# Two decoder layers on one core: early attention scores in the second layer, residual rows of the output projection written by ScalarE, and a block table for the compressed scores

## The chip, the core and the metric

The kernel runs on one core of one Trainium2 chip. A core has five engines that run their own instruction streams and meet at semaphores: TensorE (PE in the profile, with its weight loads as PEld), VectorE (DVE), ScalarE (ACT), GpSimd (POOL) and SyncE (SP), which here only issues DMAs. The metric is the time of one execution on the device in microseconds (us). Before the change the median of three runs is 758.22 us (757.21 to 758.95).

## The reference, cut to what matters

There are 256 tokens of width 1024 and two layers. Each layer is a token mixer followed by a mixture of 16 experts, and after each of the two stands a layer norm of `alpha * x + sublayer(x)`, with alpha = 4 ** 0.25.

```python
# layer 0: 16 heads of 64; keys and values in 4 groups
o_cmp = softmax(q @ kc^T, masked) @ vc     # kc, vc: 15 compressed blocks of keys and values for each group
o_slc = softmax(q @ ks^T, causal) @ vs     # all selected blocks are taken at this length
o_win = softmax(q @ kw^T, causal) @ vw     # the window covers all keys at this length
mix   = (g0 * o_cmp + g1 * o_slc + g2 * o_win) @ w_out
# layer 1: 16 heads, causal attention over one block
mix   = softmax(q @ k^T, causal) @ v @ w_out
# both layers
x = layer_norm(alpha * x + mix)
x = layer_norm(alpha * x + grouped_moe(x))     # two experts of 16 for each token, router by group
```

## The kernel before, in words

The tokens lie in two tiles of 128 rows. Weights stream through a ring of eight slots in SBUF (and a ninth place); SyncE issues each load when the slot's last user has signalled. The order in which SyncE issues is one fixed list: the projection weights of layer 0, its output weights, the first six expert matrices, then, after the output projection has freed its slots, the rest of the experts; layer 1 in the same way.

**Projection.** A unit is 512 columns of a projection weight, in eight chunks of 128 rows (index j). ScalarE rounds a chunk into a high part (`split_hi`, L1086), VectorE forms the low part (`split_lo`, L1416), and TensorE multiplies both (`project`, L579 to L581: six matmuls a chunk). There are three buffers of high and low parts, so a split waits until the chunk three before it has been used. In layer 1 the last unit (i == 5 in the loops) makes the second half of the values. After each unit two rotated tiles are transposed by TensorE (L618) and copied by ScalarE (`tr_copy`, L1099). The first half of the values is copied out of PSUM by ScalarE (`values`, L1215), the second half by VectorE (L1758).

**Attention.** The work is a row of items, 12 in layer 0 and 8 in layer 1, and every engine goes through them in a fixed order written out by hand. For each item m: TensorE writes the mask (L640) and adds the scores (L652) in two PSUM banks; VectorE takes the maximum (`attention_max`, L1465); ScalarE takes the exponential with its sum (L1235); VectorE makes the coefficient (`coefficients`, L1499); GpSimd scales the probabilities (L1348); TensorE transposes them (`transpose_probs`, L666) into PSUM banks 4 and 5; VectorE copies them to SBUF (L1748); TensorE multiplies by the values (`times_v`, L691 in layer 0, L696 in layer 1); VectorE collects the finished heads (`collect`, L1516 to L1519). In step m of its loop TensorE does scores(m), times_v(m - 3), transpose_probs(m - 2) and mask(m + 1). In layer 1 the masks and scores of items 0 and 1 are put ahead of the last chunk (j == 7) of the last unit.

**The compressed branch of layer 0** is woven into the first steps: at step 1 `compressed_scores` (L719) computes 32 small products, for each token tile, head pair and head: 64 rows of queries against 16 compressed keys. VectorE takes the maximum and subtracts it (L1473, L1474), ScalarE exponentiates (L1244), VectorE scales at step 2 (`compressed_scale`, L1480 to L1486, five instructions), TensorE transposes at step 3 (L728), VectorE copies at step 4 (L1490), and `times_compressed` (L704) adds the product to the heads' bank from step 4 on.

**The output projection's weights of layer 0** are split for w = 0 and 1 and j = 0 to 5 during the attention: ScalarE rounds (L1241), GpSimd (L1351) or VectorE (L1765) makes the low part.

**Output projection** (`mix_out`). Banks 0 to 3 hold tile a and half w. First `seed` (L784) writes alpha times the residual rows into each bank by a product with a scaled identity, at the two steps after the last item; one such product is two PE instructions. Then 8 products per bank add the projection: in layer 0 the first six as three fast products of split operands each (L777 to L779), the last two, and all eight of layer 1, as plain fp32 products (L774, two PE instructions each). At the third step after the last item TensorE does the first six of bank 0 in one go, before times_v of the last item:

```python
elif m < n + T:
    pe.wait_ge(L.exp, base[l].exp + m - 1)
    for w in range(2):
        seed(2 * (m - n) + w, m - n, w, False)
else:
    mix_out(l, 0, 0, range(0, 6))
```

Then come layer norm, routing and eight pairs of experts (`experts`), where the same kind of identity product (L784) puts the residual rows in banks 4 to 7.

Of the kernel before, what the change touches and what calls it, by code (L numbers as in the profile page):

```python
# [90 lines left out]
def build(nc, x, consts, w_in0, w_out0, cmp_kw1, cmp_kw2, cmp_vw1, cmp_vw2, cmp_kpos, cmp_vpos,  # L91
          w_in1, w_out1, router_w, router_b, w_gate, w_up, w_down, ln_g, ln_b, ln_cols, out):
    ctx = ExitStack()
    with ctx:
# [84 lines left out]
        kcT = R4[:, D + 768:D + 832]  # L179
# [58 lines left out]
        wo_hi, wo_lo = sem("wo_hi"), sem("wo_lo")  # L238
        bconst, blank = sem("bconst"), sem("blank")
# [118 lines left out]
        ITEMS = [12, 8]  # L358
        tile_of = lambda l, m: min(m % 3, 1) if l == 0 else m % T
# [23 lines left out]
        def wo_chunks(l, m):  # L383
            first = sum(WO_AT[:m])
            return list(enumerate(WO))[first:first + WO_AT[m]] if l == 0 else []

# [157 lines left out]
        def _(pe):  # L544
# [15 lines left out]
            def project(l, i):  # L560
# [64 lines left out]
            def mask(l, m):  # L625
                B = base[l]
                t, n, many = tile_of(l, m), keys(l, m), segs(l, m)
                if m == 0:
                    pe.wait_ge(L.tr_copied, B.tr_copied + (5, 8)[l])
                    pe.wait_ge(bconst, 3)  # L630
# [38 lines left out]
            def times_v(l, m):  # L669
# [30 lines left out]
                last.then_inc(L.pv, 1)  # L700

            def times_compressed(jq):
                pe.wait_ge(c_t_sb, 1)
                mm(ps[:, 6 + jq // 2 % 2, jq % 2 * S:(jq % 2 + 1) * S],  # L704
                   vblk[jq // 4][:, 2 * (jq % 4):2 * (jq % 4) + 2].rearrange("p i c -> p (i c)"), PTc[:, jq // 4, :],
                   start=False, stop=True, skip_group_check=True)

            def compressed_scores():
                pe.wait_ge(kct_sb, 1)
                pe.wait_ge(v_blocks, 1)  # L710
                for a in range(2):
                    mm(ps[:, 6 + a, 0:T * P], identb[:, :], bc(cmaskb[:, :, :], 2, H // 2), start=True, stop=False,
                       skip_group_check=True)
                for t in range(T):
                    for jq in range(H // 2):
                        for a in range(2):
                            h, g = slice(64 * a, 64 * a + 64), 2 * (jq // 4) + a
                            at = t * P + jq * CS
                            last = mm(ps[:, 6 + a, at:at + CS], qT[h, jq, t * P:(t + 1) * P], kcT[h, g * CS:(g + 1) * CS],  # L719
                                      start=False, stop=True, skip_group_check=True)  # L720
# [10 lines left out]
            def attention(l):  # L731
# [3 lines left out]
                for m in range(n + 3):  # L735
# [13 lines left out]
                    if 2 <= m < n + 2:  # L749
                        transpose_probs(l, m - 2)  # L750
                    if l == 0 and m == 3:
                        compressed_probs_transposed()
                    if l == 0 and m >= 4:
                        g, r = divmod(m - 3, 3)
                        if r == 0 or r == 1 and g == 0:
                            times_compressed(2 * g)
                        if r == 1:
                            times_compressed(2 * g + 1)
                    if (0, 1)[l] <= m < n - 1:
                        mask(l, m + 1)  # L760

            def mix_out(l, a, w, js):
                B, u = base[l], OUT[2 * l + w]
                if l == 0 and a == 0 and w == 0 and js.start == 0:
                    pe.wait_ge(wo_lo, len(WO))
# [199 lines left out]
            pe.wait_ge(blank, 2)  # L965
# [112 lines left out]
        def _(act):  # L1078
# [67 lines left out]
            for l in range(2):  # L1146
                B, C = base[l], rbase[l]
                def x_hi(a, ws=range(2)):
# [25 lines left out]
                if l == 0:  # L1174
# [36 lines left out]
                    copy(kcT, ps[:, 7, 256:320]).then_inc(kct_sb, 1)  # L1211
                else:
# [12 lines left out]
                n = ITEMS[l]  # L1225
                for m in range(n):
                    act.wait_ge(L.mx, B.mx + m + 1)
                    if m >= 2 and (l == 0 or m % T == 0):
                        act.wait_ge(L.pt, B.pt + m - 1)
                    if m >= 4 and l and m % T:  # L1230
                        act.wait_ge(L.pt, B.pt + m - 3)
                    k = keys(l, m)
                    for a in range(2):
                        for x in range(segs(l, m)):
                            last = nc.scalar.activation(probs(l, m)[:, a, x], ps[:, score_bank(l, m) + a, x * k:(x + 1) * k], ACT.Exp,  # L1235
                                                        bias=nmax[:, m % 2, a, x:x + 1],
                                                        accum_out=sums[:, m % 3, a, x:x + 1])
                    last.then_inc(L.exp, 1)
# [58 lines left out]
        def _(pool):  # L1297
# [36 lines left out]
            step(nc.gpsimd.memset(half, -0.5))  # L1334
            for l in range(2):
# [10 lines left out]
                for m in range(ITEMS[l]):  # L1346
                    pool.wait_ge(L.coef, B.coef + m + 1)
                    tt(probs(l, m), probs(l, m), bc(coef[:, m % 3, :, 0:segs(l, m)], 3, keys(l, m)), ALU.mult).then_inc(L.scaled, 1)  # L1348
                    for n, (w, j) in wo_chunks(l, m)[:1]:
                        pool.wait_ge(wo_hi, n + 1)  # L1350
                        tt(wo_lo_at(w, j), in_slot(("unit", OUT[w]))[:, j * UNIT:(j + 1) * UNIT], WO_HI[w][j],  # L1351
                           ALU.subtract).then_inc(wo_lo, 1)
# [37 lines left out]
        def _(dve):  # L1390
# [78 lines left out]
            def compressed_less_max():  # L1469
                dve.wait_ge(c_scored, 1)  # L1470
                scores_ = ps[:, 6:8, 0:T * P].rearrange("p a (k n) -> p a k n", n=CS)
                pairs = lambda v: v.rearrange("p (k a) -> p a k", a=2)
                step(nc.vector.tensor_reduce(pairs(cmax), scores_, AX.X, ALU.max, negate=True))  # L1473
                tt(Pc.rearrange("p (k a n) -> p a k n", a=2, n=CS), scores_, bc(pairs(cmax), 3, CS), ALU.add  # L1474
                   ).then_inc(c_less, 1)
# [218 lines left out]
            nc.vector.memset(identb[:, :], 0.0).then_inc(blank, 1)  # L1694
            nc.vector.memset(causalb[:, :], 0.0).then_inc(blank, 1)
            for l in range(2):
# [48 lines left out]
                for m in range(n + 4):  # L1745
                    if 3 <= m < n + 3:
                        dve.wait_ge(L.pt, B.pt + m - 2)
                        copy(probs_t(l, m - 3), ps[:, 4:6, 0:segs(l, m - 3) * keys(l, m - 3)]).then_inc(L.pt_sb, 1)  # L1748
                    if l == 0 and m == 4:
# [5 lines left out]
                    if l == 1 and m == 1:  # L1755
# [5 lines left out]
                    if l == 0 and m == 2:  # L1761
                        compressed_scale()
                    for c, (w, j) in wo_chunks(l, m - 1)[1:] if 1 <= m <= n else []:
                        dve.wait_ge(wo_hi, c + 1)
                        tt(wo_lo_at(w, j), in_slot(("unit", OUT[w]))[:, j * UNIT:(j + 1) * UNIT], WO_HI[w][j],  # L1765
                           ALU.subtract).then_inc(wo_lo, 1)
# [79 lines left out]
```

## Time and profile before

| | us |
|---|---|
| median of three runs | 758.22 |
| the profiled execution | 758.38 |
| its span | 756.6 |
| TensorE busy in it | 728.7 (96%) |
| VectorE, ScalarE, GpSimd busy | 295.8, 189.7, 109.2 |

The granted TensorE clock of the profiled execution is 0.995 of full speed. The page cuts the span into 40 slices of some 19 us. The DMA row of it is near 9 tenths in slices 1 to 5, near nothing in slices 6 and 7 (layer 0's attention), high through the experts, low again in slices 26 to 28 (layer 1's attention), and high to the end. On the time axis: layer 0's projections to about 84 us, its attention to 147, output projection and routing to 182, experts to 391; layer 1's projections to 470, its attention to 499, output projection and routing to 538, experts to the end.

### The profile page before, as it was taken

To read this page: it belongs to the slowest core of one execution; us is meant where nothing else is said; L and a number is where in the kernel's file an instruction comes from. 1 tells how busy PE (TensorE), PEld (TensorE's weight loads), DVE (VectorE), ACT (ScalarE), POOL (GpSimd) and SP (SyncE) were. 2 spreads that over 40 slices of the span, in tenths; PEclk is the share of its full clock that TensorE was granted. 3 is DMA by queue.
4 is the path that set the end of the run, shared out by engine and by line. 5 is a ranking of instruction groups with operands and counts; after the bars stand their busy time and mean duration, and the time that the engine had idled before them with its cause. 6 is when DMAs were issued, how large, how long until landed. Compare 5 with 4: busy or idle time off the path is not lost.

```text
span 756.6 us, 9076 instructions
## 1 busy us (share of the span) xinstructions
PE 728.7 (96%) x3740; PEld 391.6 (52%) x3740; DVE 295.8 (39%) x532; ACT 189.7 (25%) x435; POOL 109.2 (14%) x88
## 2 busy tenths in 40 slices
PE   8999978999999999999999999999999999999994
PEld 4877755676343443443247887646534344434331
DVE  4384788456221212121155786625421212112114
ACT  5343657133101101110132546503210111011001
POOL 0011267312000000000023230501200000000001
PEclk9999999999999999999999999999999999999997
DMA  9999800137999999999999976014799999999992
GB/s 329 299 381 424 351 1 1 57 112 272 379 407 432 426 426 427 427 427 421 422 395 386 407 287 223 1 56 158 302 376 422 429 426 429 428 429 427 420 421 112
DMA packets 42700, 245.06 MB, mean 324 GB/s; under 512 B 5920, under 2 KB 10144, under 8 KB 29344
## 3 DMA queue, kind: packets, MB, share of 16 engines
q1 hardware_dynamic: 42656, 244.43, 80.2%
q8 instruction: 32, 0.52, 0.3%
q14 instruction: 12, 0.10, 0.0%
HBM read 243.37 MB, written 1.05 MB: 323 GB/s over the span
## 4 chain that ended last, share of the span: by engine, by line
PE 79%; DMA 9%; DVE 7%; ACT 2%; issue 1%; POOL 1%; SPq 0%; DVEq 0%; ACTq 0%
PE ps L854 25%; PE ps L875 13%; DMA ring<-in_w_up 7%; PE ps L774 5%; PE ps L579 4%; PE ps L581 4%; PE ps L580 4%; PE ps L839 3%; PE ps L885 3%; PE ps L666 2%; PE ps L784 2%; PE ps L691 1%; DMA ring<-in_w_in 1%; PE ps L830 1%; PE ps L652 1%
## 5 line engine op out<-in xcount | busy, mean ns | idle before, releaser
L854 PE MATMUL ps<-ring,R 128*64 128x512 f32 x928 | 227.1, 595 | 0.0
L854 PEld LDWEIGHTS ps<-ring,R 128*64 128x64 f32 x928 | 70.2, 137 | 108.8 <-issue 107.2
L875 PE MATMUL ps<-ring,R 128*64 128x512 f32 x448 | 113.6, 596 | 0.0
L1108 ACT ACTIVATE wh<-ps,small 128x512 fp32r<-128x512 f32 x32 | 22.0, 688 | 264.4 <-PE ps L875 262.8
L1416 DVE TENSOR_TENSOR wl_r<-ring,wh 128x512 fp32r<-128x512 f32 x72 | 55.7, 792 | 41.4 <-ACT wh L1086 41.0
L875 PEld LDWEIGHTS ps<-ring,R 128*64 128x64 f32 x448 | 35.1, 137 | 67.1 <-issue 64.0
L1642 DVE SCALAR_TENSOR_TENSOR wl_r<-ps,small,wh 128x512 fp32r<-128x512 f32 x32 | 24.0, 751 | 104.8 <-ACT wh L1108 104.1
L579 PE MATMUL ps<-wh,xh_r 128*128 128x512 f32 x144 | 57.3, 398 | 1.1 <-DVE wl_r L1416 1.0
L1631 DVE TENSOR_TENSOR R<-R,ps 128x512 f32<-128x512 f32 x16 | 17.2, 1074 | 104.3 <-PE ps L854 104.3
L1086 ACT CAST wh<-ring 128x512 fp32r<-128x512 f32 x72 | 44.5, 623 | 51.5 <-PE ps L581 50.7
L581 PE MATMUL ps<-wh,xl 128*128 128x512 f32 x144 | 56.2, 390 | 0.0
L580 PE MATMUL ps<-wl_r,xh_r 128*128 128x512 f32 x144 | 56.1, 390 | 0.0
L1314 POOL TENSOR_TENSOR R<-wh,small 128x512 f32<-128x512 f32 x8 | 8.4, 1048 | 281.8 <-PE ps L860 266.8
L1638 DVE TENSOR_SCALAR wl_r<-ps 128x256 fp32r<-128x256 f32 x16 | 6.8, 425 | 104.5 <-PE ps L860 104.5
L1235 ACT ACTIVATE R<-ps,small 128x128 f32<-128x128 f32 (+1 forms) x96 | 39.1, 427 | 25.1 <-PE ps L666 17.9
L854 PE MATMUL ps<-R 128*64 128x512 f32 x96 | 42.9, 596 | 2.4 <-DMA ring<-in_w_up 2.4
L1348 POOL TENSOR_TENSOR R<-R,small 128x1024 f32<-128x1024 f32 (+1 forms) x20 | 34.5, 1726 | 45.6 <-DVE small L1499 25.3
L1340 POOL TENSOR_TENSOR R<-R 128x512 f32<-128x512 f32 (+1 forms) x16 | 22.9, 1434 | 109.1 <-DVE R L1459 109.1
L774 PE MATMUL ps<-ring,R 128*128 128x512 f32 x80 | 36.2, 595 | 0.0
L1105 ACT ACTIVATE R<-ps 128x512 f32<-128x512 f32 x16 | 9.6, 597 | 99.9 <-PE ps L854 99.9
L579 PEld LDWEIGHTS ps<-wh,xh_r 128*128 128x128 f32 x144 | 27.0, 188 | 8.8 <-DVE wl_r L1416 3.0
L581 PEld LDWEIGHTS ps<-wh,xl 128*128 128x128 f32 x144 | 27.0, 188 | 5.8
(219 smaller groups left out, 1001.7 us busy)
## 6 DMA issues: line engine op xcount, KB each, us to landing
ring<-in_w_gate SPq DMA_DIRECT2D x28, 2048.0 KB, 17.8
ring<-in_w_up SPq DMA_DIRECT2D x22, 2048.0 KB, 18.0
ring<-in_w_down SPq DMA_DIRECT2D x22, 2048.0 KB, 20.3
ring<-in_w_in SPq DMA_DIRECT2D x21, 1024.0 KB, 14.2
ring<-in_w_out SPq DMA_DIRECT2D x8, 1024.0 KB, 15.0
R<-in_w_up SPq DMA_DIRECT2D x4, 2048.0 KB, 17.5
R<-in_w_down SPq DMA_DIRECT2D x4, 2048.0 KB, 19.2
ring<-in_w_gate SPq DMA_DIRECT2D x8, 1024.0 KB, 25.5
```

What stands on the lines that cost most here:

```text
L579: mm(to, xh[:, j, tok], wh[:, c % WBUF], start=(j == 0), stop=False)
L580: mm(to, xh[:, j, tok], wl[:, c % WBUF], start=False, stop=False)
L581: last = mm(to, xl[:, j, tok], wh[:, c % WBUF], start=False, stop=(j == KJ - 1))
L774: last = mm(to, OT[j][:, tok], in_slot(("unit", u))[:, j * UNIT:(j + 1) * UNIT], start=False, stop=(j == KJ - 1), skip_group_check=True)
L854: last = mm(ps[64 * e:64 * e + 64, to, :], xe[:, j, at + 64 * e:at + 64 * e + 64], slots[e][:, j * UNIT:(j + 1) * UNIT], start=(j == 0), s ...
L875: last = mm(ps[64 * e:64 * e + 64, 2 + w, :], hT[:, k, 64 * e:64 * e + 64], slots[e][:, at:at + UNIT], start=(k == 0), stop=(k == FJ - 1))
L1086: copy(wh[:, c % WBUF], in_slot(("unit", u))[:, j * UNIT:(j + 1) * UNIT]).then_inc(w_hi, 1)
L1235: last = nc.scalar.activation(probs(l, m)[:, a, x], ps[:, score_bank(l, m) + a, x * k:(x + 1) * k], ACT.Exp, bias=nmax[:, m % 2, a, x:x + ...
L1340: tt(stage[r % 2][:, 0:n], stage[r % 2][:, 0:n], rope_b[r % 2][:, 0:n], ALU.add).then_inc(L.roped, 1)
L1348: tt(probs(l, m), probs(l, m), bc(coef[:, m % 3, :, 0:segs(l, m)], 3, keys(l, m)), ALU.mult).then_inc(L.scaled, 1)
L1416: tt(wl[:, c % WBUF], in_slot(("unit", u))[:, j * UNIT:(j + 1) * UNIT], wh[:, c % WBUF], ALU.subtract).then_inc(w_lo, 1)
L1642: stt(Yp[1][w], ps[:, 2 + w, :], slot_gate, Yp[0][w], ALU.mult, ALU.subtract).then_inc(rd.y_lo, 1)
```

## The change

Four edits, of which the last word of the title, "experts' identity products kept", says that `seed` stays in the experts.

1. **Residual rows by ScalarE.** After the exponentials of each layer's last two items ScalarE writes alpha times two half rows from SBUF into PSUM banks that those exponentials have just freed. TensorE's four `seed` products per layer go, and the first six products of bank 0 are spread over the three steps after the last item, two at each, all ahead of that step's times_v. `mix_out` waits for `seeded`, and in layer 0 for the low parts of its own half only. In layer 1, item 6 used only half of each of its two banks; two small products with the mask fill the other half there.
2. **Early scores in layer 1.** In the last unit, masks and scores of items 0, 1 and 2 go ahead of chunks 2, 4 and 6, and transpose_probs of item 0 ahead of chunk 7. ScalarE copies the first values at chunks 0 and 1 and does the exponentials of items 0 and 1 after the splits of chunks 4 and 6; VectorE does the maxima of items 0 and 1 after the splits of chunks 3 and 5, and the coefficient of item 0 after chunk 7. The loops then begin at item 2 or step 3.
3. **Compressed scores by a block table.** The compressed keys are kept in a table with zeros off the blocks, so that one product over 128 rows and 32 columns serves two heads: 16 products in one bank in place of 32 in two.
4. **The rest of the compressed branch** moves a step later: scale at step 3, transposes at step 4, copy and first products at step 5.

```diff
+        EARLY_SCORES = [2, 4, 6]
# project(l, i)
-                    if l and i == 5 and j == KJ - 1:
-                        mask(1, 0)
-                        mask(1, 1)
-                        scores(1, 0)
-                        scores(1, 1)
+                    if l and i == 5:
+                        if j in EARLY_SCORES:
+                            mask(1, EARLY_SCORES.index(j))
+                            scores(1, EARLY_SCORES.index(j))
+                        if j == KJ - 1:
+                            transpose_probs(1, 0)
                     pe.wait_ge(w_lo, c + 1)
# scores(l, m)
+                if (l, m) == (1, ITEMS[1] - T):
+                    for a in range(2):
+                        mm(ps[:, score_bank(l, m) + a, segs(l, m) * n:UNIT], identb[:, :], bc(causalb[:, :], 1, 2), start=False, stop=True,
+                           skip_group_check=True)
# compressed_scores
-                for a in range(2):
-                    mm(ps[:, 6 + a, 0:T * P], identb[:, :], bc(cmaskb[:, :, :], 2, H // 2), start=True, stop=False,
-                       skip_group_check=True)
+                mm(ps[:, 6, :], identb[:, :], bc(cmaskb[:, :, :], 2, H), start=True, stop=False, skip_group_check=True)
                 for t in range(T):
                     for jq in range(H // 2):
...
+                        at = (t * H + 2 * jq) * CS
+                        last = mm(ps[:, 6, at:at + 2 * CS], qT[:, jq, t * P:(t + 1) * P], kcT[:, jq // 4].rearrange("p a n -> p (a n)"),
+                                  start=False, stop=True, skip_group_check=True)
# attention(l), TensorE
+                else:
+                    transpose_probs(1, 1)
+                    mask(1, 3)
+                for m in range(3 * l, n + 3):
                     if m < n:
-                        if l == 0 or m >= T:
-                            scores(l, m)
-                    elif m < n + T:
-                        pe.wait_ge(L.exp, base[l].exp + m - 1)
-                        for w in range(2):
-                            seed(2 * (m - n) + w, m - n, w, False)
+                        scores(l, m)
                     else:
-                        mix_out(l, 0, 0, range(0, 6))
+                        mix_out(l, 0, 0, range(2 * (m - n), 2 * (m - n) + 2))
...
-                    if l == 0 and m == 3:
+                    if l == 0 and m == 4:
                         compressed_probs_transposed()
# ScalarE
+                            if i == 5 and j in (0, 1):
+                                values(j)
                             if i == 5 and j in (4, 6):
-                                values(j // 2 - 2)
+                                exponentials(j // 2 - 2)
...
+                    if m >= ITEMS[l] - T:
+                        a = m - ITEMS[l] + T
+                        act.wait_ge(L.exp, B.exp + m + 1)
+                        for w in range(2):
+                            nc.scalar.activation(ps[:, 2 * a + w, :], X[:, a, w * UNIT:(w + 1) * UNIT], ACT.Copy, scale=ALPHA
+                                                 ).then_inc(seeded, 1)
# VectorE
+                            if i == 5 and j in (3, 5):
+                                attention_max(1, j // 2 - 1)
+                    coefficients(1, 0)
...
+                for m in range(T * l, n + 4):
+                    if 3 + l <= m < n + 3:
+                        copy_probs_t(m - 3)
...
-                    if l == 1 and m == 1:
+                    if l == 1 and m == 2:
+                        copy_probs_t(0)
...
-                    if l == 0 and m == 2:
+                    if l == 0 and m == 3:
                         compressed_scale()
```

## Rows read from the trace of the kernel before

**Rows 1.** The page, the chain that ended last, share of the span by engine:

```profile
PE 79%; DMA 9%; DVE 7%; ACT 2%; issue 1%; POOL 1%; SPq 0%; DVEq 0%; ACTq 0%
```

**Rows 2.** Stretches: us; busy PE, PEld, DVE, ACT, POOL; PEclk; DMA share; GB/s:

```profile
134.00:147.50 13.50, 13.50 (x87) 9.08 (x85) 5.51 (x7) 2.44 (x9) 5.92 (x4) 1.00 0.23 79
...
183.00:346.00 163.00, 162.82 (x786) 65.71 (x786) 31.63 (x46) 17.76 (x27) 4.53 (x4) 1.00 0.98 409
...
499.00:516.00 17.00, 17.00 (x61) 8.36 (x61) 5.11 (x9) 2.25 (x4) 0.55 (x1) 1.00 0.01 3
```

**Rows 3.** Waits of SyncE's queue: us in total, times, longest:

```profile
SPq L435 <- PE ps L774: 57.2, 4, 21.5
```

**Rows 4.** The chain in order of time: start, us, what, pieces:

```profile
81.83 1.04 PE ps L1021 x8
...
111.20 1.01 PE ps L691 x8
...
134.07 1.72 PE ps L784 x4
...
162.15 1.69 PE ps L799 x16
...
346.26 28.31 DMA ring<-in_w_up
...
490.53 1.72 PE ps L784 x4
...
493.86 5.15 PE ps L774 x12
```

**Rows 5.** Timeline, end of layer 0's attention: start, us, instruction [idle before it, releaser]:

```profile
134.17 0.47 ACT L1235 ACTIVATE R<-ps,small 128x256 f32<-128x256 f32 x1 [1.32 <-PE ps L666]
...
142.07 1.22 DVE L1748 COPY R<-ps 128x1024 f32<-128x1024 f32 x1 [2.73 <-PE ps L666]
...
142.12 0.58 PE L777 MATMUL ps<-xh_r,R_r 128*128 128x512 f32 x1
...
146.51 0.85 PEld L691 LDWEIGHTS ps<-R 128*64 128x64 f32 x16 [0.35 <-issue]
```

**Rows 6.** Groups by line and form, ScalarE: busy, mean ns, idle before:

```profile
L1086 ACT CAST wh<-ring 128x512 fp32r<-128x512 f32 x72 | 44.5, 623 | 51.5 <-PE ps L581 50.7 <-DMA ring<-in_w_in 0.8
```

**Rows 7.** Timeline, last projection unit of layer 1 and start of its attention:

```profile
456.85 0.47 PE L579 MATMUL ps<-wh,xh_r 128*128 128x512 f32 x1
...
464.62 1.28 ACT L1235 ACT_TABLE_LOAD   x1
464.63 0.69 DVE L1416 TENSOR_TENSOR wl_r<-ring,wh 128x512 fp32r<-128x512 f32 x1 [0.67 <-ACT wh L1086]
...
468.55 0.50 PE L579 MATMUL ps<-wh,xh_r 128*128 128x512 f32 x1
...
468.67 1.23 DVE L1465 TENSOR_REDUCE small<-ps 128x4 f32<-128x1024 f32 x1 [0.17 <-PE ps L652]
...
469.93 0.47 ACT L1235 ACTIVATE R<-ps,small 128x256 f32<-128x256 f32 x1
...
470.32 1.04 POOL L1348 TENSOR_TENSOR R<-R,small 128x512 f32<-128x512 f32 x1 [16.40 <-DVE small L1499]
...
471.93 0.17 DVE L1499 RECIPROCAL small<-small 128x4 f32<-128x4 f32 x1
...
475.26 1.22 DVE L1748 COPY R<-ps 128x1024 f32<-128x1024 f32 x1 [0.46 <-PE ps L666]
```

**Rows 8.** Timeline, ScalarE in layer 0's routing:

```profile
163.52 1.28 ACT L1267 ACT_TABLE_LOAD   x1
...
164.88 0.22 ACT L1267 ACTIVATE small<-small 128x16 f32<-128x16 f32 x1
```

**Rows 9.** Timeline, first steps of layer 0's attention:

```profile
87.64 3.75 PE L719 MATMUL ps<-R 64*128 64x16 f32 x64
...
98.33 1.08 PE L691 MATMUL ps<-R 128*64 128x256 f32 x8 [3.04 <-DVE R L1748]
```

More of the change, by code:

```diff
@@ L237, in build @@
         cmpw_used = sem("cmpw_used")
[L238 to L239 removed]
+        wo_hi, wo_lo_pool, wo_lo_dve = sem("wo_hi"), sem("wo_lo_pool"), sem("wo_lo_dve")
+        seeded = sem("seeded")
+        bconst = sem("bconst")
         out_done = sem("out_done")
@@ L385, in wo_chunks, with wo_lo_counts @@
             return list(enumerate(WO))[first:first + WO_AT[m]] if l == 0 else []
+        def wo_lo_counts(ws):
+            own = [[c for c in wo_chunks(0, m) if c[1][0] < ws] for m in range(ITEMS[0])]
+            return sum(len(c[:1]) for c in own), sum(len(c[1:]) for c in own)
         block = ctx.enter_context(nc.Block())
@@ L699, in times_v @@
                                           start=(r == 0 and i == 0), stop=False, skip_group_check=True)
-                last.then_inc(L.pv, 1)
+                if l or m != 2:
+                    last.then_inc(L.pv, 1)
             def times_compressed(jq):
                 pe.wait_ge(c_t_sb, 1)
-                mm(ps[:, 6 + jq // 2 % 2, jq % 2 * S:(jq % 2 + 1) * S],
+                last = mm(ps[:, 6 + jq // 2 % 2, jq % 2 * S:(jq % 2 + 1) * S],
                    vblk[jq // 4][:, 2 * (jq % 4):2 * (jq % 4) + 2].rearrange("p i c -> p (i c)"), PTc[:, jq // 4, :],
                    start=False, stop=True, skip_group_check=True)
+                if jq == 1:
+                    last.then_inc(L.pv, 1)
             def compressed_scores():
-                pe.wait_ge(kct_sb, 1)
+                pe.wait_ge(kct_sb, 2)
                 pe.wait_ge(v_blocks, 1)
-                for a in range(2):
-                    mm(ps[:, 6 + a, 0:T * P], identb[:, :], bc(cmaskb[:, :, :], 2, H // 2), start=True, stop=False,
-                       skip_group_check=True)
+                mm(ps[:, 6, :], identb[:, :], bc(cmaskb[:, :, :], 2, H), start=True, stop=False, skip_group_check=True)
                 for t in range(T):
                     for jq in range(H // 2):
[L716 to L720, printed above, removed]
+                        at = (t * H + 2 * jq) * CS
+                        last = mm(ps[:, 6, at:at + 2 * CS], qT[:, jq, t * P:(t + 1) * P], kcT[:, jq // 4].rearrange("p a n -> p (a n)"),
+                                  start=False, stop=True, skip_group_check=True)
                 last.then_inc(c_scored, 1)
@@ L763, in mix_out @@
                 B, u = base[l], OUT[2 * l + w]
-                if l == 0 and a == 0 and w == 0 and js.start == 0:
-                    pe.wait_ge(wo_lo, len(WO))
+                if js.start == 0:
+                    pe.wait_ge(seeded, 2 * T * l + 2 * a + w + 1)
+                    if l == 0 and a == 0:
+                        by_pool, by_dve = wo_lo_counts(w + 1)
+                        pe.wait_ge(wo_lo_pool, by_pool)
+                        pe.wait_ge(wo_lo_dve, by_dve)
                 pieces = PIECED if l == 0 else 0
@@ L1147, in _, with exponentials @@
                 B, C = base[l], rbase[l]
+                def exponentials(m):
+                    act.wait_ge(L.mx, B.mx + m + 1)
+                    if m >= 2 and (l == 0 or m % T == 0):
+                        act.wait_ge(L.pt, B.pt + m - 1)
+                    if m >= 4 and l and m % T:
+                        act.wait_ge(L.pt, B.pt + m - 3)
+                    k = keys(l, m)
+                    for a in range(2):
+                        for x in range(segs(l, m)):
+                            last = nc.scalar.activation(probs(l, m)[:, a, x], ps[:, score_bank(l, m) + a, x * k:(x + 1) * k], ACT.Exp,
+                                                        bias=nmax[:, m % 2, a, x:x + 1],
+                                                        accum_out=sums[:, m % 3, a, x:x + 1])
+                    last.then_inc(L.exp, 1)
                 def x_hi(a, ws=range(2)):
@@ L1210, in _ @@
                     act.wait_ge(kct, 1)
-                    copy(kcT, ps[:, 7, 256:320]).then_inc(kct_sb, 1)
+                    for a in range(2):
+                        h = slice(64 * a, 64 * a + 64)
+                        copy(kcT[h, :, a], ps[h, 7, 256:320].rearrange("p (u a n) -> p u a n", u=2, a=2)[:, :, a]).then_inc(kct_sb, 1)
                 else:
@@ L1221, in _ @@
                                 tr_copy(1, 2 * (i - 2) + j - 1)
+                            if i == 5 and j in (0, 1):
+                                values(j)
                             if i == 5 and j in (4, 6):
-                                values(j // 2 - 2)
[L1225 to L1238, printed above, removed]
+                                exponentials(j // 2 - 2)
+                for m in range(T * l, ITEMS[l]):
+                    exponentials(m)
                     for _, (w, j) in wo_chunks(l, m):
@@ L1334, in _ @@
             step(nc.gpsimd.memset(half, -0.5))
+            step(nc.gpsimd.memset(kcT, 0.0))
             for l in range(2):
@@ L1470, in compressed_less_max @@
                 dve.wait_ge(c_scored, 1)
[L1471 to L1475, printed above, removed]
+                scores_ = ps[:, 6, :].rearrange("p (h n) -> p h n", n=CS)
+                step(nc.vector.tensor_reduce(cmax, scores_, AX.X, ALU.max, negate=True))
+                tt(Pc.rearrange("p (h n) -> p h n", n=CS), scores_, bc(cmax, 2, CS), ALU.add).then_inc(c_less, 1)
             def compressed_scale():
@@ L1744, in _, with copy_probs_t @@
                 n = ITEMS[l]
[L1745 to L1749, printed above, removed]
+                def copy_probs_t(m):
+                    dve.wait_ge(L.pt, B.pt + m + 1)
+                    copy(probs_t(l, m), ps[:, 4:6, 0:segs(l, m) * keys(l, m)]).then_inc(L.pt_sb, 1)
+                for m in range(T * l, n + 4):
+                    if 3 + l <= m < n + 3:
+                        copy_probs_t(m - 3)
+                    if l == 0 and m == 5:
                         compressed_copy()
```

23 lines of the change are left out of this document (11 added, 12 removed).

## The prediction

> **What bounds the kernel now.** I read the chain of waits first: 79% of it is TensorE, 9% DMA, 7% VectorE [rows 1]. The second view is the busy time by stretch. At the end of layer 0's attention TensorE is busy 13.50 of 13.50 us, in layer 1's output projection 17.00 of 17.00, through layer 0's experts 162.82 of 163.00 [rows 2]. In the experts the DMA is also at 0.98 [rows 2] and the chain ends that stage in a transfer of 28.31 us [rows 4], so both limits are close together there. What matters is whether an earlier start moves the transfers too. In layer 1's output projection the DMA stands at 0.01 [rows 2]; SyncE sits there until TensorE's output products free a slot, up to 21.5 us in one wait [rows 3]. The loads that feed the experts are thus released by the work that this change brings forward, so I let a gain ahead of the experts pass to the end in full. The third view is the timeline around the edited places.
>
> **Layer 0, end of the attention.** The four identity products leave TensorE. Two of them last 1.72 us in the chain (x4, two instructions each) [rows 4], and there are two such pairs: 3.44. The first six products of bank 0 stay, 18 instructions from 142.12 to 0.35 before 146.51 [rows 5], 4.05 us or 0.23 each; now 6 of them (1.35) stand at each of the three steps where 1.72, 1.72 and 4.05 stood. TensorE's sum falls by 3.44. Can times_v of the last item use it? It also waits for VectorE's copy, which starts at 142.07 and lasts 1.22 [rows 5], so at 143.3 at the earliest if that copy does not move, in place of 146.5: 3.2. The transposes ahead of that copy come a few tenths sooner, since the two earlier steps are 0.37 shorter each. I take 3.3, between 3.0 and 3.5. What is late next is that copy, by no more than 0.2.
>
> ScalarE takes over 4 writes of 512 columns. A pass over 512 columns from SBUF lasts 0.62 [rows 6]; writing with a scale into PSUM is not in the trace, and between 0.5 and 0.8 holds it. Two of them, 1.25, fall where ScalarE idles 1.32 before the last item's exponentials [rows 5]; the other two come after those, where it has nothing to do. Behind the writes on ScalarE's queue stands only that exponential; late by 0.3 at worst, and its result is transposed only two steps on. I count 0, up to +0.3. `mix_out` now waits for them: the first two are written before TensorE gets to its place at 134.1. SyncE and GpSimd lose and gain nothing.
>
> **Layer 1, end of the attention.** The pairs of identity products are 1.72 again [rows 4]; six plain products of bank 0 take 5.15 in one go ahead of the last times_v [rows 4], so two take 1.72. The two steps after the last item keep their length (1.72 for 1.72), and the third shrinks from 5.15 to 1.72: 3.43. VectorE's copy of 1.22 runs beside it and is shorter than 1.72, so TensorE stays the limit. ScalarE's 1.25 between the exponentials of items 6 and 7 could push the latter back, 0 to 1.25; its transposes lie behind both steps of products, so I take 0. The two small mask products that fill the banks of item 6 are 0.2 to 0.4 of TensorE in a step that waits for VectorE anyway: 0. Sum 3.4, between 2.6 and 3.5.
>
> **Layer 1, start of the attention.** Here I expect a loss. A chunk is six products of 0.23 (the pitch of rows 5), 1.38. From 456.85 to 468.55 [rows 7] there are seven chunks (9.65) and masks and scores of items 0 and 1, 2.05; I split these 0.95 and 1.1, as item 0 has half the keys, and item 2 is like item 0. On the old clock:
> - TensorE: chunks 0 and 1 to 459.6, item 0 to 460.55, chunks 2 and 3 to 463.3, item 1 to 464.4, chunks 4 and 5 to 467.15, item 2 to 468.1, chunk 6 to 469.5.
> - Transposes of item 0 now stand before chunk 7. They need: VectorE's maximum of item 1 (1.23), ScalarE's exponential of item 1 (469.93 to 471.93, 2.0) [rows 7], the high split of chunk 7 (0.62) [rows 6], the low split (0.69), the coefficient (0.17), GpSimd's scaling (1.04) [rows 7]. The maximum and the exponential of item 1 are in this chain only because the split of chunk 7 is queued behind them on ScalarE, and the coefficient of item 0 behind that on VectorE. Together 5.75, with six handovers of some 0.05 6.05: from 464.4 to 470.45.
> - TensorE stands 470.45 - 469.5 = 0.95 before them. Behind it are four transposes (0.52, at 0.13 a piece [rows 4]) and chunk 7: it ends at 472.35, against 469.95 before, 2.4 later.
> - Then transposes of item 1 (1.04), mask and scores of item 3 (1.4 with a pause), its maximum (1.23), a coefficient (0.17), and only then VectorE's copy of item 1's transposes: 476.3 with handovers, against 475.26 [rows 7]. Before, that copy came as soon as its transposes were there.
>
> So the steady steps begin 1.1 to 1.4 later; I take +1.3. Bounds: no wait at all for the item-0 transposes, and the copy not held, gives -0.7; both doubled, +3.3. The first exponential and its table load (1.28) [rows 7] stand after the split of chunk 4, and have until chunk 5's low part is wanted at 465.8; ScalarE would be through at about 463.8. The two value copies moved ahead cost ScalarE 1.2 while three buffers are full: 0 to +0.5.
>
> The page ScalarE: Activation LUTs of the Trainium skill (What ACT_TABLE_LOAD costs) speaks against this place: a switch to another set is a load of about 1.28 us and a drain of about as much again, 2.66 in all. In this trace a load begins at 163.52 and lasts 1.28, and the next activation begins at 164.88 [rows 8], 0.08 after it: no drain is to be seen. By the page's figure the exponential of item 0 and with it the splits of chunks 5 and 6 would come some 1.4 later, and the sum below would be about 1 us less of a gain; I go by the row.
>
> **Layer 0, start of the attention.** The compressed scores last 3.75 as 64 pieces of 64 rows, 0.058 each [rows 9]. Now 32 pieces of 128 rows by 32 columns: the nearest rows are 16 columns at 0.106 and 64 columns at 0.13 [rows 4], so 3.4 to 4.15, taken as 3.65: -0.1, between -0.4 and +0.4. The page TensorEngine Tiling (Theoretical Speedup) has a contraction over at most 64 rows up to 2x faster in tiles, so by it the fused form gives up the factor it saves in count; the rows agree, and the edit is worth nothing by either.
>
> Moving `compressed_scale` one step later takes away the wait of 3.04 before the first times_v [rows 9], but its VectorE time then stands before the next copy, and the first products with the compressed values, 1 us that lay in such a wait, move to a step that the chain shows as TensorE pieces back to back around 111.20 [rows 4]. I carry 0.2 of gain past that step; between -0.6 (loss) and 1.2.
>
> **Sum.** -3.3 - 3.4 + 1.3 - 0.2 = -5.6. The profiled execution takes 758.38; 752.8. The median of 758.22 is 0.16 lower, inside the spread of its three runs; I keep 752.8.
>
> **Rivals.**
> 1. The early scores cost nothing (TensorE never waits for the item-0 transposes). For it: the chain of 6.05 has 5.1 of TensorE work beside it; against: the queue order above. -3.3 - 3.4 - 0.5 = -7.2: 751.2. Chance 0.15.
> 2. The wait at chunk 7 is two to three times as long, through a later exponential or late splits: start +3.0, sum -3.9: 754.5. Chance 0.17.
> 3. Layer 0's gain is swallowed by the transfers that end its experts: for it, the 28.31 us transfer and DMA at 0.98; against, the loads wait for TensorE. Only layer 1 counts: -3.4 + 1.3 = -2.1: 756.3. Chance 0.08.
> 4. Slower: the splits starve. If both chains in the last unit lie open, since ScalarE's exponentials stand ahead of the splits of chunks 5 to 7, TensorE waits 6.05 for the second and, for the first, 4.7: table load 1.28, two splits 1.3, and maximum and exponential of an item with half the keys, which I estimate at 0.65 of item 1's, 2.1. With the 1.3 that I have already it costs some 11: -6.9 + 11 = +4: 762.5. It decides from 7 us lost in the last unit. Three buffers and 1.38 a chunk as cover speak against it. Chance 0.04.
> 5. The four edits do not do what they say at the two ends: the writes come late and TensorE waits for them. The writes' queue place speaks against it; with both ends at half, -3.35 + 1.1 = -2.2: 756.2. Chance 0.04.
>
> **Numbers.** My forecast of 752.8 has a chance of 0.52, with 751.8 to 754.0 for itself. With rivals 1 and 2 the range is 750.9 to 755.9, which leaves some 0.2 outside. A measurement can tell 0.2%, 1.5 us, from no change. Faster by more than that, under 756.7: the forecast, rivals 1 and 2 and much of 3 and 5, 0.88. Within it 0.08, slower 0.04.
>
> **What would show it.** In the profile after, ahead of the experts no identity products remain, and three groups of two products stand before the last three times_v of either layer; times_v of the last item begins right after its copy in layer 0 and after the products in layer 1. In layer 1 TensorE has a gap of about 1 us before chunk 7 of the last unit, released by GpSimd, and VectorE's copy of item 1 follows the maximum of item 3 without a pause. The first wait of 3.04 in layer 0 is gone, a shorter one stands a step later. The experts' stages keep their length. The prediction is wrong if the experts get longer by what the front gave, or if TensorE waits in the last unit for a split.

## The result, and the profile after

The changed kernel takes 762.27 us (median of 5 runs, 760.18 to 763.91), the kernel before beside it 758.73 (5 runs, 757.21 to 759.77): ratio 1.0041, 95% interval 1.0022 to 1.0059. It is slower by 0.4%, where 752.8 was forecast. The profiled execution took 760.18, its span 758.4 against 756.6 before; it is the fastest of the five, and the account below is of it alone.

What the four edits were to do is in the trace. The residual rows are written by ScalarE in two pairs of 0.57 each, VectorE's last copy moves up, and the last times_v of layer 0 begins at 143.16 (timeline, end of layer 0's attention; start, us, instruction):

```profile
132.63 1.14 ACT L1267 ACTIVATE ps<-X 128x512 f32<-128x512 f32 x2
...
136.40 1.14 ACT L1267 ACTIVATE ps<-X 128x512 f32<-128x512 f32 x2
...
141.45 1.23 DVE L1773 COPY R<-ps 128x1024 f32<-128x1024 f32 x1 [2.21 <-PE ps L677]
...
142.85 0.39 PE L791 MATMUL ps<-xh_r,R_r 128*128 128x512 f32 x1
143.16 1.09 PE L702 MATMUL ps<-R 128*64 128x128 f32 x16
```

Before, that product began at 146.51 [rows 5]: 3.35 sooner. It stands right behind the last of the six products (L791); the copy had ended 0.5 before it. The experts then keep their length, and their last transfer starts 3.30 sooner and lasts the same 28.3 [rows 2, 4]. By stretch (us; busy PE, PEld, DVE, ACT, POOL; PEclk; DMA share; GB/s):

```profile
134.00:144.30 10.30, 10.22 (x79) 7.57 (x79) 5.51 (x7) 3.46 (x11) 5.83 (x4) 1.00 0.19 40
179.70:342.70 163.00, 162.81 (x786) 65.74 (x784) 31.61 (x46) 17.70 (x27) 4.49 (x4) 1.00 0.98 408
501.20:518.00 16.80, 16.80 (x60) 8.35 (x60) 5.11 (x9) 2.24 (x4) 0.55 (x1) 1.00 0.18 56
```

All is lost in the 12 us that follow layer 0's experts, a place that the prediction does not mention. The chain of waits there, first in the kernel after (start, us, what, pieces):

```profile
342.96 28.30 DMA ring<-in_w_up
...
386.55 1.19 PE ps L897 x4
387.74 5.99 issue
393.73 5.31 PE ps L564 x14
```

and in the kernel before, where the same warm-up products of layer 1 are line 558:

```profile
391.07 0.18 issue
391.25 3.20 PE ps L558 x14
```

There TensorE had stood only 0.2 us. After, it stands for 6 us in "issue", time in which the engine waited for nothing that the profile shows. While it stands the granted clock falls from 1.00 to 0.50 (1.2 GHz in place of 2.4) and is back by 399 us, so the same 14 products take 5.31 instead of 3.20. Stretches of the kernel after (us; busy PE, PEld, DVE, ACT, POOL; PEclk; DMA share; GB/s):

```profile
387.00:389.00 2.00, 0.74 (x4) 0.27 (x2) 1.71 (x5) 1.66 (x4) 1.75 (x2) 1.00 1.06 388
391.00:392.00 1.00, 0.00 (x0) 0.00 (x0) 0.69 (x2) 0.38 (x1) 1.00 (x2) 0.61 1.05 385
392.00:393.00 1.00, 0.00 (x0) 0.00 (x0) 0.00 (x0) 0.00 (x0) 0.77 (x1) 0.50 1.06 393
395.00:396.00 1.00, 1.00 (x4) 0.43 (x3) 0.00 (x0) 0.00 (x0) 0.00 (x0) 0.50 1.06 389
398.00:399.00 1.00, 1.00 (x7) 0.57 (x6) 0.00 (x0) 0.00 (x0) 0.00 (x0) 0.98 1.03 379
```

and one of the kernel before, in which these products run:

```profile
392.00:393.00 1.00, 1.00 (x7) 0.41 (x6) 1.00 (x2) 0.47 (x2) 1.00 (x2) 1.00 1.04 381
```

The account of the span: -3.3 at the end of layer 0's experts (387.74 against some 391.07), +5.8 stall, +2.1 half clock, -2.4 from there to the end of layer 1's attention, -0.4 in what follows: +1.8.

What stands at that place in the code is the branch around the spare rounds, `pe.If(most > SLOTS)`: it is taken, across 296 instructions of TensorE's compiled program. One queue of the trace (q8) has 32 transfers in all, 0.52 MB, so 16 KB each; TensorE's compiled program is 8149 instructions in 0.52 MB, so this is taken to be its program arriving, 256 instructions at a time. Between 357 and 390.9 us the kernel after has none of these, only one of another queue (q14), and between 390.9 and 393, while TensorE stands, it has one (packets, MB, share):

```profile
q14 instruction: 1, 0.01, 0.1%
```

```profile
q8 instruction: 1, 0.02, 3.3%
```

The kernel before has its fetch between 381 and 391, ahead of the branch:

```profile
q8 instruction: 1, 0.02, 0.7%
```

Its compiled program has the branch as TensorE's instruction 4116, the changed one as 4036: in layer 0 the block table takes away 32 products and one mask, the identity products 8, each a weight load and a product, and two waits were added. That is 80 fewer. The Trainium skill, Runtime: NRT & Kernel Launch (Instruction fetch mechanics), says that engines fetch their program in blocks of 256 instructions, in sequence, and that a taken branch to a block outside the window waits for a fetch. The trace agrees on the block, 16 KB a transfer.

### The profile page after: what moved, and what is told of

The parts are those of the page before. It is cut to its first block, busy times and chain, and to the rows that moved or that the text cites. A ratio compares the mean times of both kernels' runs of the same rounds, so it can differ in the third digit from the quotient of the medians.

```text
span 758.4 us, 8995 instructions
## 1 busy us (share of the span) xinstructions
PE 726.2 (96%) x3693; PEld 389.7 (51%) x3693; DVE 295.3 (39%) x532; ACT 193.4 (26%) x444; POOL 109.2 (14%) x89
## 4 chain that ended last, share of the span: by engine, by line
PE 79%; DMA 8%; DVE 7%; issue 2%; ACT 2%; POOL 1%; SPq 0%; DVEq 0%; ACTq 0%
PE ps L866 25%; PE ps L887 13%; DMA ring<-in_w_up 7%; PE ps L786 5%; PE ps L586 3%; PE ps L588 3%; PE ps L587 3%; PE ps L851 3%; PE ps L897 3%; PE ps L663 2%; PE ps L677 2%; PE ps L702 1%; PE ps L842 1%; DMA ring<-in_w_in 1%; DVE R L1454 1%
```

## The experiments

Each ratio is to runs of the kernel before taken beside that kernel (medians 760.49, 760.12 or 760.17).

Theory 1: the change lost its gain because it moved the branch in the blocks of the program. Theory 2: TensorE stands there because it arrives 3.3 us sooner, at transfers that are late. Further down, theory 3 on the clock and theory 4 on the early scores. The instructions added below are waits on a semaphore long reached, spread over layer 0's projections (the compiler joins them in twos, so 144 waits are 80 instructions):

```diff
+            def idle_waits(i, j):
+                k = (1, 2, 3, 4).index(i) * 8 + j
+                for _ in range((k + 1) * 144 // 32 - k * 144 // 32):
+                    pe.wait_ge(ident_in, 16)
...
                 for j in range(KJ):
...
+                    if l == 0 and i in (1, 2, 3, 4):
+                        idle_waits(i, j)
                     pe.wait_ge(w_lo, c + 1)
```

**e1: the changed kernel, branch back at 4116 by 80 waits.**

> The changed kernel with 80 instructions that do nothing (waits on a semaphore that has long been reached) spread over TensorE's projections of layer 0, so that the jump over the spare rounds at the end of layer 0 stands at instruction 4116 of TensorE's program, as in the kernel before, instead of 4036. All work is unchanged. Theory 1 (the 6.0 us in which TensorE stands at that jump come from the jump's place in the blocks of 256 instructions in which the program is fetched): no stall before layer 1's warm-up products, which take 3.2 us at full clock instead of 5.3, and a time about 8 us below the changed kernel, 752 to 754.5. Theory 2 (the stall comes from reaching the jump 3.3 us earlier, while the transfers of layer 1's first weights or the register read are late): the stall stays at 5 to 6 us, and the time is 760 to 762.5. If the added waits themselves cost something, it shows before 130 us.

Measured: 755.16 against 760.49, ratio 0.9932 (0.9902 to 0.9963). The stall is 0.2, the warm-up products take 3.20. Same work, no stall: theory 2 falls, and e10 below, which reaches the branch sooner still than the kernel after (386.57 against 387.74) and does not stand, bears it out. The median lies just above the expected range; falls of the clock, which come under e3, are in its profile too (0.62 at 102 to 104 us).

**e2: the kernel before, branch moved to 4292.**

> The kernel before with 176 such instructions in the same place: its jump then stands at 4292, which is the changed kernel's 4036 plus one block of 256, and its work is unchanged. Theory 1: TensorE now stands about 6 us at the jump at the end of layer 0 in the kernel before too, the warm-up products after it take about 5.3 us instead of 3.2, and the time is about 766 (8 us more). Theory 2 (arrival time, transfers): no stall, 758 to 759. If so many added waits cost time of their own, the layer 0 projections (20 to 84 us) become longer, which the windows would show apart.

Measured: 767.88 against 760.49, ratio 1.0091 (1.0064 to 1.0119), 7.4 more. The kernel before now stands too, in the chain:

```profile
392.16 5.93 issue
```

The 14 products behind it take 5.38. Its windows from 20 to 84 us are unchanged (TensorE busy 62.66 of 64 against 62.90), and its compressed scores begin at 87.37 in the chain against 87.70, so the waits themselves cost nothing. Theory 1 holds in both directions.

**e5, e10, e11: how far the branch must move.** The same edit with 29, 40 and 53 instructions.

> The changed kernel with 29 instead of 80 added instructions, so that the jump at the end of layer 0 stands at 4065. In the kernel before, the block fetch ahead of its jump began at 383.4 us, 7.9 us and some 65 to 75 instructions before the jump at 4116, so about instruction 4041 to 4055. Theory 1 in this form (the block with the jump's target is asked for when TensorE passes that instruction, and the stall is what the fetch then still lacks): it is asked for 10 to 24 instructions, 1 to 2.5 us, ahead of the jump, and the stall is shorter than 6.0 but not gone, 2.5 to 5 us. Rival (it is all or nothing): 0.2 or 6.0 us.

> The changed kernel with 40 added instructions: the jump stands at 4076. The stall was 6.0 us with the jump at 4036, 5.5 at 4065 and 0.2 at 4116. Theory 1 with the block asked for at some instruction just below 4065 and the stall being what the fetch then still lacks, at about 0.1 to 0.15 us an instruction: 3.5 to 5 us here. Rival (all or nothing, with the 0.5 us of before only scatter): 5.5 to 6.0 or 0.2.

> As before with 53 added instructions, the jump at 4089: by theory 1 another 13 instructions, 1.3 to 2 us, less: 1.5 to 3.5 us of stall, and a clock that falls less or not at all after it. Rival: 5.5 to 6.0 or 0.2.

Measured, one run each: 761.49, 751.13 and 751.74 us. With the branch at 4065 the stall is 5.5, at 4076 and 4089 it is 0.2. The chain of e5:

```profile
389.89 5.53 issue
395.42 4.63 PE ps L564 x14
```

and of e10, whose fetch came before the branch:

```profile
385.39 1.19 PE ps L904 x4
386.57 0.20 issue
386.77 3.20 PE ps L564 x14
```

My graded form of theory 1 is wrong, the rival right: eleven instructions decide between all and nothing. The transfer records of the traces show why nothing lies between: in all three stalls the transfer begins only 3.4 (after), 3.4 (e2) and 2.9 us (e5) after TensorE came to stand, lasts 1.1, and TensorE goes on some 1.5 after its end. What is paid is a whole fetch, not the rest of one under way. That it is asked for only then fits an arithmetic of these figures: with blocks of 256 and a jump of 296, the target is two blocks on only when the branch stands in the last 40 places of its block. If a block ends between 4065 and 4076, and so again 256 later, the branch stands there at 4036, 4065 and 4292, and does not at 4076, 4089 and 4116. All six places agree; no run tried the other edge, below 4036, so this form of the rule is inferred and not shown. e10 is, in its one run, the change as it was meant, undisturbed: 9.0 us below the profiled execution after, of which 5.8 are the stall, 2.1 the half clock behind it, and 1.2 come from layer 0.

**e3: without the block table.** Theory 3 is on the granted clock of layer 0's attention: in the kernel after it falls to 0.50 at 91 to 94 us, right behind the block table's products; before it did not.

```diff
-                        at = (t * H + 2 * jq) * CS
-                        last = mm(ps[:, 6, at:at + 2 * CS], qT[:, jq, t * P:(t + 1) * P], kcT[:, jq // 4].rearrange("p a n -> p (a n)"),
+                        for a in range(2):
+                            h, g = slice(64 * a, 64 * a + 64), 2 * (jq // 4) + a
+                            at = t * P + jq * CS
+                            last = mm(ps[:, 6 + a, at:at + CS], qT[h, jq, t * P:(t + 1) * P], kcT[h, g * CS:(g + 1) * CS],
...
```

Edit 4, the compressed branch a step later, stays in this kernel and in e6.

> The changed kernel with the compressed scores computed as before, by 64 products on half the rows instead of 32 with the block table, and 14 waits so that the jump stands at 4116 as in e1. Theory 3 (the block table's products are what lowers the granted clock to 0.50 at 91 to 94 us): the clock stays at 1.00 from 84 to 98 us, the products take 3.7 us instead of 3.5, the scores and transposes right behind them 1.1 and 1.1 instead of 2.1 and 1.5, and the time is 0.2 to 0.6 below e1. Rival (the clock falls for another reason there, as the wait on the scaled rows): the fall stays, and the time is 0.0 to 0.3 above e1.

Measured: 755.64, ratio 0.9923 (0.9893 to 0.9954), not to be told from e1. The fall is there all the same, and longer (0.50 from 90 to 96 us); theory 3 falls. e2, with the work of before, has it too, and e6 below. Granted clock (PEclk) in e2 and in e6:

```profile
91.00:96.00 5.00, 5.00 (x24) 2.75 (x24) 4.45 (x8) 2.54 (x10) 2.87 (x2) 0.66 0.06 23
```

```profile
90.00:96.00 6.00, 6.00 (x34) 4.06 (x33) 2.90 (x6) 2.39 (x9) 1.90 (x1) 0.50 0.15 63
104.00:110.00 6.00, 5.28 (x32) 4.48 (x34) 4.04 (x7) 1.57 (x7) 3.51 (x2) 0.50 0.00 0
```

e9 to e12 show none. The falls come and go between executions: e1, e7, e10 and e11 have the same products in layer 0's attention, and e1 and e7 show a fall at 102 to 106 us, e10 and e11 none.

**e4 and e6: the edits apart.** e4 undoes the early scores, e6 the block table as well; branch at 4116.

```diff
-                        if j in EARLY_SCORES:
-                            mask(1, EARLY_SCORES.index(j))
-                            scores(1, EARLY_SCORES.index(j))
...
+                    if l and i == 5 and j == KJ - 1:
+                        mask(1, 0)
+                        mask(1, 1)
+                        scores(1, 0)
+                        scores(1, 1)
...
```

> The changed kernel with layer 1's early scores as before (both items of the first pair ahead of the last chunk, their exponentials after the unit), and 80 waits as in e1, with the jump at 4116. Theory 4 (the early scores only cost: TensorE waits about 0.5 us for the exponential ahead of the first transposes, and the probabilities' second copy came 1.0 us later): 0.7 to 1.3 below e1. Rival (the early scores take the first items off the chain of layer 1's attention, which the later items then keep): the time is 0.5 to 2 above e1.

> The changed kernel with the early scores and the block table undone: of the change there is left the residual rows written by ScalarE with the identity products gone; 14 waits put the jump at 4116. By the runs so far: no stall, layer 1 from its start to the end as in e4 (361.9 us from the first warm-up product to the end, against 365.3 before), and a time 7 to 8 us below before, within 0.8 of e4's ratio (0.987 to 0.991). Rival (the block table is worth more than that): 1 us or more slower than e4 against before, 0.990 to 0.993.

Measured: e4 752.53, ratio 0.9887 (0.9861 to 0.9914); e6 755.18, ratio 0.9930 (0.9901 to 0.9960). e6's ratio lies in the range of its rival, but its six runs fall in two groups by the clock: 750.38 at a mean granted clock of 0.995, the other five 755.02 to 755.41 at 0.985 to 0.989. By medians neither expectation on the block table can be judged. For layer 1 the timeline can be, from its first warm-up product to the end of its last attention product, where the granted clock of these kernels is 1.00: 108.79 before; 106.40, 106.37 and 106.40 with the early scores (e1, e10, e11); 105.66, 105.42 and 105.39 without (e4, e6, e12). In layer 1 the residual rows by ScalarE are worth 3.3 (3.1 to 3.4), the early scores cost 0.9 (0.7 to 1.0). Theory 4 holds.

**e7 and e8: what the early scores cost.** e7 puts the first early transposes behind the last chunk; e8 moves one copy on VectorE:

```diff
                 for m in range(T * l, n + 4):
-                    if 3 + l <= m < n + 3:
+                    if l == 1 and m == 3:
+                        copy_probs_t(1)
+                    if (3, 5)[l] <= m < n + 3:
                         copy_probs_t(m - 3)
...
```

> e1 with the first early transposes moved from ahead of the last chunk of layer 1's last unit to behind it. If TensorE's wait ahead of that chunk is what the early scores cost, the wait goes (0.3 to 0.5 us on the path), and layer 1 from its first warm-up product to the end takes 362.5 against 363.0 in e1 and 361.9 in e4. Rival (the cost is VectorE's order: the second copy of the probabilities stands behind the maximum of item 3, which waits for that item's scores): nothing is won, 362.9 to 363.3.

> e1 with one change in VectorE's order in layer 1: the second copy of the transposed probabilities goes ahead of the maximum of item 3. In e1 VectorE takes that maximum from 473.1 to 474.3 us, after a wait for item 3's scores, and copies at 474.4, though the transposes were done at 471.7; TensorE waits 1.0 us for the copy. Theory (this order is the cost of the early scores): the copy comes about 1.2 us earlier, TensorE's 1.0 us wait goes, and layer 1 from its first warm-up product to the end takes 361.8 to 362.3 instead of 363.0, as e4 (361.9) or less. Rival (the maximum of item 3, then 1.1 us later, is what the next products wait for): 362.8 to 363.5.

Measured: e7 (one run) 752.81, and 363.8 from the first warm-up product to the end, no gain: the rival, with more loss than it gave. TensorE's wait moved behind the chunk, where the second transposes wait 0.87 for the copy of the first:

```profile
469.19 1.06 PE L682 MATMUL ps<-cst,R 128*128 128x128 f32 x8 [0.87 <-DVE R L1779]
```

e8: 752.15, ratio 0.9896 (0.9880 to 0.9913), 362.2 to the end, in the range of the theory. VectorE in e1 and then in e8:

```profile
473.10 1.23 DVE L1497 TENSOR_REDUCE small<-ps 128x4 f32<-128x1024 f32 x1 [1.56 <-PE ps L670]
474.24 0.17 DVE L1529 RECIPROCAL small<-small 128x4 f32<-128x4 f32 x1
474.32 1.20 DVE L1780 COPY R<-ps 128x1024 f32<-128x1024 f32 x1
```

```profile
471.84 1.23 DVE L1780 COPY R<-ps 128x1024 f32<-128x1024 f32 x1 [0.21 <-PE ps L684]
473.19 1.23 DVE L1497 TENSOR_REDUCE small<-ps 128x4 f32<-128x1024 f32 x1
```

The copy fits into the 1.56 in which VectorE waited for scores, and TensorE's waits for it fall from 1.4 in two to 0.2. It is mostly the order on VectorE that cost, and with it mended the early scores still win nothing over e4.

**e9 and e12: warm-up products in a wait.** Both are e4 with ten more. This is e9; e12 has `m == 4`:

```diff
+                    if l == 0 and m == 3:
+                        keep_warm(7, 10)
                     if m >= 3:
                         times_v(l, m - 3)
```

> e4 with ten warm-up products (0.21 us each at full clock) put into the 3.1 us in which TensorE waits for the scaled compressed rows, at about 102 us in layer 0. Theory (the second fall of the clock, 98 to 110 us in e1 to e4, follows this idle wait): in the profile the clock stays at 1.00 after 100 us, and the time is 0.5 to 1.5 us below e4 (ratio to before 0.986 to 0.988). Rival (the falls come from the small products ahead of the wait and stay as they are): the same falls, and a time within 0.5 us of e4 or above it by the products that no longer fit in the gap.

> e9's ten warm-up products stood one item too early, ahead of products that did not wait, so that they were work on the path (2.3 us of it in the chain) and not in the gap. Here they stand one item later, in the 3.1 us in which TensorE waits for the second copy of the probabilities at about 98 to 101 us of layer 0. Theory (the second fall of the clock, at 101 to 111 us, follows this wait): no fall there in the profile, the products of layer 0's attention after it not longer than at full clock, and a time 0.5 to 2 us below e4 (ratio to before 0.985 to 0.988). Rival (the falls come from the small products ahead): the falls stay, and the ratio is that of e4 within 0.001.

Measured: e9 753.31, ratio 0.9926 (0.9900 to 0.9952), a miss: there was no wait at that step, and 2.27 us of products came onto the path. e12: 750.81, ratio 0.9882 (0.9865 to 0.9898), the best median here. Its wait:

```profile
98.44 2.33 PE L564 MATMUL ps<-causalb,identb 128*128 128x512 bf16 x10
101.66 1.09 PE L708 MATMUL ps<-R 128*64 128x128 f32 x16 [0.89 <-DVE R L1774]
```

All four of its runs have a clock of 0.994 or 0.995, those of e4 0.989 to 0.994. This speaks for the theory, but the first fall (90 to 96 us), which stands ahead of the products, is missing as well, and the ratio is within 0.001 of e4's, as the rival had it. It is not shown.

## Why the prediction was wrong

- **The step that failed** is in its first part: "I let a gain ahead of the experts pass to the end in full." Through the experts it did (3.3 at 387.74). Then the branch behind them took 5.8 more than before and the clock after it 2.1. I priced removed products by their time alone; their number, 80 instructions with the waits, moved a branch from 4116 to 4036, where its target is not fetched in time. That is a term of +7.9 that the sum lacks, and none of the five rivals is it: rival 4 has the time (762.5) by luck, for no split starved.
- **Layer 0's end**, -3.3: -3.35 in the profile after, 0.1 of it won before 128 us. The limit at the last times_v is the products, not the copy as I had it. The writes cost ScalarE 0.57 each and nobody waited for them.
- **Layer 0's start**, -0.2: the block table takes 3.49 in the chain, against 3.65 foreseen. In the kernel after, the half clock at 91 to 94 us took the lead: scores behind the table 2.08 instead of 1.13, transposes 1.53 instead of 1.09, and by 128 us it is only 0.1 ahead. Without a fall (e10) the times_v that begins at 128.20 before begins at 126.57: this term is 1.6 and not 0.2, and layer 1 starts 4.5 sooner (4.3 in e11), where my two terms make 3.5. The long wait did not go, it moved: times_v of the second item waits 3.2. But it is the only one left up to 112 us, where before there were two, 4.3 in all. No run has edit 4 apart from the rest.
- **Layer 1's end**, -3.4: 3.3 by the timelines of e4, e6 and e12.
- **Layer 1's start**, +1.3: 0.9 by the same. Of the two parts foreseen one was there. TensorE is idle 0.32 ahead of the item-0 transposes, not 0.95, and the kernel before was idle 0.30 ahead of its own, so this part is next to nothing. The second copy stands directly behind the maximum of item 3, as foreseen; e8, where this order is mended, takes 0.7 of the 0.9 away (105.7 against 106.4). First the kernel before, then after:

```profile
471.42 0.66 PE L666 MATMUL ps<-cst,R 128*128 128x128 f32 x4 [0.30 <-POOL R L1348]
```

```profile
475.38 0.66 PE L677 MATMUL ps<-cst,R 128*128 128x128 f32 x4 [0.32 <-POOL R L1373]
...
479.72 1.23 DVE L1490 TENSOR_REDUCE small<-ps 128x4 f32<-128x1024 f32 x1 [1.56 <-PE ps L663]
480.86 0.17 DVE L1522 RECIPROCAL small<-small 128x4 f32<-128x4 f32 x1
480.94 1.20 DVE L1773 COPY R<-ps 128x1024 f32<-128x1024 f32 x1
```

  Against the unit's start the copy is 1.0 later than before [rows 7], as worked out.
- **The sum**, -5.6 or a ratio of 0.9929 to the median of before: e1 has 0.9932, which is in part luck: its runs have falls of the clock in layer 0 (mean granted clock 0.987 to 0.992). e10, without one, has a span of 749.3 against 756.6, which is 7.3 less: 4.5 ahead of layer 1, 2.4 from there to the end of layer 1's attention, 0.3 behind it. The edits' own times were priced within the range, 1.7 short of that run; what they did to the program's layout was not priced at all.

## What to carry to other kernels

An edit that changes how many instructions an engine has ahead of a taken branch moves the branch in the blocks in which the program arrives, and here that cost more (7.9) than the edits gave; look at the fetch queue and at "issue" around each branch before trusting a sum of durations, and move the branch by a few idle waits where it stalls. A fast path that jumps over code is such a branch, even if that code never runs, as here. And judge parts by the timeline between two fixed events where the clock is level, not by medians that differ by less than the executions of one kernel do.

## What the runs showed of the hardware

- A taken branch whose target had not been fetched cost 5.5 to 6.0 us on TensorE (three kernels), and 0.2 where it had been. The fetch began 3.4 us into the stall in the kernel after, lasted 1.1, and TensorE went on 1.5 after its end. The granted clock was 0.50 from 392 to 398 us, in the stall and behind it.
- The condition is sharp: the branch stalls at 4065 and not at 4076, and at 4292 it stalls again.
- In layer 0's attention the granted clock fell to 0.50 for 3 to 7 us at 89 to 98 and again at 98 to 111 us in some executions and not in others of the same work. In the first of the two the busy view shows TensorE busy throughout (6.00 of 6.00 us in e6 from 90 to 96). Which of them fall stays open.
- Redundant waits, 176 more instructions in layer 0's projections, cost nothing measurable there.
